# Two-layer hybrid backbone: output products in two 64-row halves, modulation columns one round later, half of two rounds' readout weights on VectorE

## The reference

```python
sh1, sc1, g1, sh2, sc2, g2 = split(silu(c) @ w_mod[layer] + b_mod[layer], 6)   # and for c_ctx
# state-space layer, per group and direction: state 64 complex, 16 channels
states = scan(lam_bar, B_bar @ u)                   # forward in time, and backward
y = real(C_fwd @ states_fwd) + real(C_bwd @ states_bwd) + d_skip * u
q, k = rope(rmsnorm(q)), rope(rmsnorm(k))           # per head, on latent tokens
```

## Time and profile before

| | |
|---|---|
| median of 3 runs | 1943.32 us (1941.05 to 1944.64) |
| profiled execution, its own time | 1942.77 us |
| span of that execution, first to last instruction | 1941.1 us |
| mean granted clock of TensorE (1 is 2.4 GHz) | 0.952 |
| busy: TensorE, weight loads, VectorE, ScalarE, GpSimd | 91%, 55%, 34%, 21%, 17% of the span |
| readout loop from z(1) to the first scores, first and second layer | 133.6 us, 115.3 us |
| chain that ended last, by engine | TensorE 61%, DMA 11%, VectorE 10%, SyncE's queue 6%, GpSimd 5% |

### The profile page before, as it was taken

One profiled execution on the slowest core, in us unless ns is written; L12 is line 12 of the kernel. 1 busy time (PEld: TensorE's weight loads), 2 busy tenths in 40 slices (PEclk: granted clock), 3 DMA queues, 4 the chain that ended last, 5 costly groups with the idle time before them and its releaser, 6 DMA issues.

```text
span 1941.1 us, 25808 instructions
## 1 busy us (share of the span) xinstructions
PE 1762.7 (91%) x9800; PEld 1064.2 (55%) x9800; DVE 656.6 (34%) x1410; ACT 411.4 (21%) x846; POOL 337.1 (17%) x314
## 2 busy tenths in 40 slices
PE   5999998889999999999979798999789999997796
PEld 2567555554444444555546446766458886554463
DVE  4669442660110113211101367775281113110012
ACT  3111111552000003222212231111152002221122
POOL 0004352870000001100000110425291000000000
PEclk9999897999999999999999898999699999999898
DMA  9313258309221243699999421144543367999992
GB/s 387 109 44 114 76 189 296 85 23 349 106 108 65 94 188 130 250 389 345 387 395 388 140 86 66 44 168 139 196 63 126 135 250 280 346 383 394 386 380 89
DMA packets 113523, 397.32 MB, mean 205 GB/s; under 512 B 42992, under 2 KB 62448, under 8 KB 74256
## 3 DMA queue, kind: packets, MB, share of 16 engines
q1 hardware_dynamic: 55920, 327.04, 43.8%
q10 hardware_dynamic: 50720, 29.54, 6.2%
q0 software_dynamic: 6784, 39.33, 6.0%
HBM read 369.65 MB, written 38.80 MB: 210 GB/s over the span
## 4 chain that ended last, share of the span: by engine, by line
PE 61%; DMA 11%; DVE 10%; SPq 6%; POOL 5%; issue 4%; ACT 2%; ACTq 1%; POOLq 0%; DVEq 0%
PE tile_ps L547 54%; SPq L492 6%; DMA arena<-sorted_in 4%; PE turn_ps L547 4%; DMA ring<-in_wpack 3%; POOL arena L1724 2%; DMA vn<-in_wpack 2%; PE out_ps L547 1%; ACTq L1086 1%; DMA arena<-arena 1%; PE turn_ps L772 1%; DVE arena L1592 1%; DVE x L1659 1%; DMA x<-in_xT 1%; DVE rstd L1365 1%
## 5 line engine op out<-in xcount | busy, mean ns | idle before, releaser
L547 PE MATMUL tile_ps<-h,ring 128*128 128x512 f32 (+1 forms) x1312 | 471.9, 514 | 3.9 <-ACT h L965 1.9
L547 PEld LDWEIGHTS tile_ps<-h,ring 128*128 128x128 f32 x1312 | 249.1, 192 | 214.1 <-issue 198.8
L547 PE MATMUL tile_ps<-arena 64*16 64x128 f32 (+4 forms) x1984 | 257.4, 376 | 31.2 <-ACT arena L1180 11.4
L547 PE MATMUL tile_ps<-arena,ring 128*128 128x512 f32 (+1 forms) x704 | 235.4, 486 | 2.7 <-issue 2.7
L547 PEld LDWEIGHTS tile_ps<-arena 128*64 128x64 f32 (+3 forms) x1984 | 165.1, 162 | 95.1 <-issue 64.9
L547 PEld LDWEIGHTS tile_ps<-arena,ring 128*128 128x128 f32 x704 | 133.9, 190 | 96.3 <-issue 87.4
L1724 POOL TENSOR_SCALAR arena<-arena,smx 128x512 f32<-128x512 f32 (+1 forms) x96 | 129.0, 1360 | 81.4 <-DVE smx L1578 81.1
L547 PE MATMUL tile_ps<-ring,arena 128*64 128x256 f32 (+1 forms) x624 | 97.4, 454 | 11.3 <-ACT arena L1180 7.1
L1156 ACT ACTIVATE arena<-tile_ps 128x512 f32<-128x512 f32 (+1 forms) x56 | 27.4, 490 | 347.4 <-PE tile_ps L547 347.4
L1650 DVE TENSOR_TENSOR arena<-tile_ps,arena 64x256 f32<-64x256 f32 x40 | 16.6, 416 | 225.0 <-ACT arena L1177 225.0
L1613 DVE TENSOR_TENSOR arena<-tile_ps,arena 128x512 f32<-128x512 f32 (+1 forms) x32 | 17.9, 558 | 212.1 <-PE tile_ps L547 212.1
(11 more groups left out here) (272 smaller groups left out, 2259.1 us busy)
## 6 DMA issues: line engine op xcount, KB each, us to landing
ring<-in_wpack SPq DMA_DIRECT2D x176, 1024.0 KB, 8.5
arena<-in_wpack SPq DMA_DIRECT2D x64, 1024.0 KB, 17.4
h<-in_wpack SPq DMA_DIRECT2D x15, 1024.0 KB, 26.0
qa<-in_wpack SPq DMA_DIRECT2D x12, 1024.0 KB, 14.7
qn<-in_wpack SPq DMA_DIRECT2D x12, 1024.0 KB, 17.1
kn<-in_wpack SPq DMA_DIRECT2D x12, 1024.0 KB, 20.0
vn<-in_wpack SPq DMA_DIRECT2D x12, 1024.0 KB, 22.1
sorted_out<-arena ACTq DMA_DIRECT2D x80, 128.0 KB, 7.5
```

Of the source, the lines that this page charges most:

```text
L547: return nc.tensor.matmul(out, lhsT, rhs, start=start, stop=stop)
```

## The change

Three things are changed.

1. The Toeplitz product of y is cut into its two halves of 64 rows: `lower` into bank `y`, `upper` into bank `yb`. Each group now has six products of 64 rows in place of one of 128 and four of 64, and the first into `yb` is no longer that with `cp`.
2. `mc` of a round's block moves to the round behind it, right after y there (in round 8, ahead of y), and `mr` moves behind the projection. The blocks of the second layer that rounds 5 to 7 make have `mr` behind the moved `mc` and their own `mc` behind that, ahead of the round's own `mr`; the one that stood in the attention moves to round 8. VectorE's and ScalarE's parts move along, and so do the banks and the order of the ring's slots.
3. For rounds 6 and 7 (`SHARED`) GpSimd makes the real part of `cp` with three products, and VectorE the imaginary part with three more of 128 x 640 (`readout_part`). z(6) and z(7) wait for both.

```diff
-IN_ROUND = {5: 0, 6: 1, 7: 2}
-IN_STEP = {1: 3}
+IN_ROUND = {5: 0, 6: 1, 7: 2, 8: 3}
+def next_mod(l, q):
+    return [IN_ROUND[q]] if l + 1 < LAYERS and q in IN_ROUND else []
+SHARED = (6, 7)
...
     # tile_jobs, the loop of rounds
             names += [(l, "z", q, 0), (l, "z", q, 1)] if q < NQ else []
-            names += [(l, "y", q - 1), (l, "yb", q - 1)] if q else []
+            late = [(l, "mc", MOD1 + q - 1)] if q else []
+            late += [(l + 1, "mr", n) for n in next_mod(l, q)]
+            out = [(l, "y", q - 1), (l, "yb", q - 1)] if q else []
+            names += out + late if q < NQ else late + out
             names += [(l, "qk_ms", q)] if q <= KW else []
+            names += [(l + 1, "mc", n) for n in next_mod(l, q)]
+            names += in_loop(fill, q)
             names += [(l, "mr", MOD1 + q)] if q < NQ else []
-            names += in_loop(fill, q)
-            names += [(l, "mc", MOD1 + q)] if q < NQ else []
             names += [(l, "rope", q)] if q <= KW else []
...
     # TensorE
+                def late_modulation(q):
+                    modulation_columns(l, MOD1 + q - 1)
+                    for n in next_mod(l, q):
+                        modulation(l + 1, n, l)
...
                         pe.wait_ge(cp_done, l * NQ + q + 1)
+                        if q in SHARED:
+                            pe.wait_ge(cp_other, l * len(SHARED) + SHARED.index(q) + 1)
...
-                            mm(bank(fwd)[:, cols], tm[:, o % 2, g, :], ug[:, G, :], True, False)
+                            for d, to in ((lower, fwd), (upper, bwd)):
+                                mm(bank(to)[:, cols], tm[d, o % 2, g, :], ug[d, G, :], True, False)
...
-                                b = mm(bank(bwd)[:, cols], co[upper], s, r == 0, r == 1)
+                                b = mm(bank(bwd)[:, cols], co[upper], s, False, r == 1)
...
     # VectorE
+            def readout_part(q):
...
+                TT(out, pv[1], cv[0], ALU.mult)
+                link(TT(tmp, pv[0], cv[1], ALU.mult))
+                TT(out, out, tmp, ALU.subtract).then_inc(cp_other, 1)
...
+                    if q + 1 in SHARED:
+                        wait_full(dve, (l, "y", q - 1))
+                        readout_part(q + 1)
...
     # GpSimd
+                    if q in SHARED:
+                        TT(o0, o0, ctmp, ALU.add).then_inc(cp_done, 1)
+                    else:
```

More of the change, by code:

```diff
@@ L158, in slot_steps @@
         steps += projected(job)
-    for q in range(NQ):
-        steps += mod(l, MOD1 + q)
+    for q in range(NQ + 1):
+        for n in next_mod(l, q):
+            steps += mod(l + 1, n)
         for job in in_loop(fill, q):
             steps += projected(job)
-        if l + 1 < LAYERS and q in IN_ROUND:
-            steps += mod(l + 1, IN_ROUND[q])
-    if l + 1 < LAYERS:
-        for n in sorted(IN_STEP):
-            steps += mod(l + 1, IN_STEP[n])
+        if q < NQ:
+            steps += mod(l, MOD1 + q)
     for kind, *at in mix_order():
@@ L732, in _ @@
                         product((l, "qk_ms", q), [(c("head_mean"), qsq[:, t:])], bank((l, "qk_ms", q))[:, t:])
-                    if q < NQ:
-                        modulation(l, MOD1 + q, l)
+                    for n in next_mod(l, q):
+                        modulation_columns(l + 1, n)
                     for job in in_loop(fill, q):
@@ L737, in _ @@
                     if q < NQ:
-                        modulation_columns(l, MOD1 + q)
+                        modulation(l, MOD1 + q, l)
                     if q <= KW:
@@ L742, in _ @@
                         product((l, "rope", q), [(c("rot"), v)], bank((l, "rope", q))[:, 0:LAT])
-                    if l + 1 < LAYERS and q in IN_ROUND:
-                        modulation(l + 1, IN_ROUND[q], l)
-                        modulation_columns(l + 1, IN_ROUND[q])
                 us = pairs[l]
@@ L761, in _ @@
                                                         qq[a:a + HD, q0:q0 + P], kk[a:a + HD, 0:nk]))
-                    early = l + 1 < LAYERS and n in IN_STEP
-                    if early:
-                        modulation(l + 1, IN_STEP[n], l)
                     if LAG <= n < len(us) + LAG:
@@ L1086, in _ @@
                             act.dma_start(tm[j * GRP:(j + 1) * GRP, q % 2], zs[:, :, a:a + P]).then_inc(tm_in, 16)
+                    if q == NQ:
+                        for n in next_mod(l, q):
+                            copy_rows(l + 1, n)
                     if q:
@@ L1093, in _ @@
                             head_squares(l, q + 1, c0)
+                    for job in in_loop(fill, q):
+                        copy_projection(job, c0)
                     if q < NQ:
                         copy_rows(l, MOD1 + q)
[L1096 to L1099 removed]
                 for q in range(NQ):
```

42 lines of the change are left out of this document (22 added, 20 removed).

## The result

The changed kernel takes 1960.13 us (median of 4 runs, 1957.76 to 1964.19) against 1943.16 us (4 runs) before: a ratio of 1.009, 95% interval 1.0071 to 1.011. It is slower by 17 us where 12 us less were forecast. Its profiled execution has a span of 1958.6 us and a mean granted clock of 0.945 (0.952 before).

A forecast was written before the change was run, and what follows sets the result against it. TensorE, busy for 91% of the span, was taken to bound the kernel. Gains of 7.5 and 8.3 us less losses of 2.4 and 1.1 gave 12.3 us less, 1931.0 us on the median; likeliest case 1924 to 1936, wider range 1918 to 1942.

The forecast's parts named there:

- The term for low clock in rounds 1 to 4: Rounds 1 to 4: 8.5 us for low clock, 6.1 in the first layer and 2.4 in the second.
- The term for the loads in the first layer's rounds 5 to 8: Two ring slots asked for earlier there: priced at nothing, and at up to 5.5 us if that fails.
- the path from z(6) to z(7) in the second layer: z(7) would come 13.5 us after z(6) in place of 16.9: 3.4 us less.
- signs named for "right": y(4) 2.7 us; projection waits over 2; first-layer rounds at least 18.6; second-layer z(6) 12 behind z(5); first transpose 8 behind scores.
- Output products: y in each round: six pairs per group take 2.7 us, 1.3 less; at low clock 5.1 in place of 6.5.
- The fourth rival: y's 64-row halves don't run side by side, so y gains 0.4 us per round: 1934 us, chance 0.04.
- The floor: Rounds 1 to 4: a round can't be shorter than 18.6 us in the first layer, 15.2 in the second.
- the second rival: Waits of 2.7 us for ScalarE's copy keep TensorE at 1.2 GHz through projection and `mr`: 1948 us, chance 0.09.
- the first rival: The clock stays up with the shorter y; rounds 1 to 4 take 74.4 and 60.0 us: 1919 us, chance 0.15.
- Rounds 5 to 8, second layer: With VectorE sharing GpSimd's products, z(6), z(7) and y(7) gain 2.9, 3.4 and 1.2 us: 7.5 us in all.
- Rounds 5 to 8, first layer: DMAs land 2.3 us earlier, path to the scores 0.8 less, block gone from attention 5.2: 8.3 us in all.
- The third rival: z(6), z(7) come early, but y's DMAs land as before and VectorE's products run beside GpSimd's: 1940 us, chance 0.14.

The follow-up runs named there:

- e1: The kernel before with only y's output product cut into two 64-row halves: 1933.33 us, against 1943 for the kernel before.
- e5: The kernel before with y in halves in both layers and VectorE's three readout products in the second layer alone: 1929.92 us.
- e6: The changed kernel without VectorE's products (`SHARED = ()`), keeping halves and late modulation: 1968.2 us, ratio 1.0105 to the kernel before.
- e7: The changed kernel with second-layer modulation blocks in rounds 5 to 8 using weights already in the ring, 8 loads of 1 MB fewer: 1946.2 us.
- e3: The changed kernel with y's 128-row product and without VectorE's products, so only the moved modulation stays: 1955.29 us.
- e2: The kernel before with only half of the readout weights of rounds 6 and 7 made on VectorE: 1940.3 us.

## Why the prediction was wrong

Three terms of the sum failed. The term for low clock in rounds 1 to 4 was 8.5 us in the two layers and measured 17.9. The term for the loads in the first layer's rounds 5 to 8, put at nothing, hid the largest miss: that stretch took 12.0 us more than forecast. And the path from z(6) to z(7) in the second layer, 13.5 us in the sum, took 19.5, since it left out a wait for the DMAs into `tm`. Most of the signs named for "right" were there even so (y, the waits for the copy, rounds of over 18.6 us, z(6) 12 us behind z(5)), and the clock of rounds 1 to 4 was 0.87 and 0.85, not 0.75 or less: the signs tested the parts that were priced, not those that were left out.

**Output products: right.** From z to `mc` or `qk_ms` are 4.7 us, not 5.8: y gives 1.1 us a round where 1.3 were forecast (2.86 for 2.7 us). At low clock y takes 5.3 us (5.1 forecast, 6.5 before). The fourth rival is out: the 48 loads of a y take less than the 40 before. Weight loads of TensorE in round 3 of the first layer:

```profile
242.15 2.76 PEld L552 LDWEIGHTS tile_ps<-arena 64*128 64x128 f32 x48 [0.21 <-issue]
```

The Trainium skill, TensorE: Matmul & The Clock Gate, section LDWEIGHTS, says that a load costs by its columns and not by its rows. For single loads the trace of the kernel before agrees: two of 64 rows, one in each half and side by side, take 0.19 us, and so does one of 128. What is out is the sum by that rule, in which each of the 48 would have its place behind the last:

```profile
276.70 0.19 PEld L547 LDWEIGHTS tile_ps<-arena 64*128 64x128 f32 x2
...
277.33 0.19 PEld L547 LDWEIGHTS tile_ps<-arena 128*128 128x128 f32 x1
```

**Rounds 1 to 4: the mechanism right, the term for low clock wrong.** The floor held: the waits for the copy are 10.3 us in four rounds (4 x 2.7 = 10.8 forecast). Above the floor of 4 x 18.6 = 74.4 us I put 6.1 for low clock, "since low clock now falls in part on idle time". Measured are 10.7. Of the 22.8 us at 1.2 GHz only 3.0 fell on idle time; the other 19.8, half of them lost, are 9.9 of the 10.7. In rounds 2 and 3 the clock fell at about the end of the wait (in round 3 from 249.9 to 253.3, and the projection begins at 250.03), in round 1 in its middle, in round 4 ahead of it, from 267.0 on, during `qk_ms`; each time the low stretch reached into the projection, the longest work of the round. In the second layer the same term was 2.4 and is 7.2 us, though some 5.4 of 20.5 fell on idle time. The four projections there take 5.38 to 5.68 us, not 3.5 to 3.7. It was the second rival's mechanism in part: the low clock took only part of each projection, and `mr` ran at full clock (1.92 us). Its price of 25.6 us is measured as 17.9, and its total of 1948 us was passed because rounds 5 to 8 lost as well.

**The step that was not taken.** The prediction found the wait and priced it, but treated the round as given. In the order of before the shorter y keeps the clock at 2.4 GHz (e1 and e5, the first rival's mechanism, worth 7.8 and 3.4 us in the profiled executions), with waits of 1.4 to 1.8 us. The late order makes them up to 3.2 us, as `mc` with 0.9 us stands where `mr` with 1.9 stood, and takes the clock away again (e6, the same halves in the late order: 19.8 and 27.3 us at 1.2 GHz). That turned the sign in rounds 1 to 4.

**Rounds 5 to 8, second layer: half right.** z(6) starts 12.1 us after z(5) (12.0 forecast), and VectorE's products for it take 0.82 us each (0.86 forecast), in the timeline of VectorE:

```profile
1372.38 0.81 DVE L1361 TENSOR_TENSOR arena<-arena 128x640 f32<-128x640 f32 x1
1373.11 0.82 DVE L1362 TENSOR_TENSOR arena<-arena 128x640 f32<-128x640 f32 x1
1373.96 0.82 DVE L1363 TENSOR_TENSOR arena<-arena 128x640 f32<-128x640 f32 x1
```

But z(6) to z(7) takes 19.5 us, not 13.5, and y(5) waits 3.95 of them for `tm`'s DMAs. I never asked what stood behind the wait on GpSimd, and what the new times of the slots do to it. Before, SyncE asked for its four loads when `tm`'s issues of round 5 had all begun; now it asks ahead of them. Timelines of ScalarE and SyncE in the second layer, with the line of the DMA view that ends in the median us from issue to landing of these eight, before:

```profile
1350.49 5.12 ACTq L1086 DMA_DIRECT2D arena<-arena  x8
1355.38 2.26 SPq L492 DMA_DIRECT2D ring<-in_wpack  x4
arena<-arena ACTq DMA_DIRECT2D x8, 32.0 KB, 2.0
```

and after:

```profile
1361.54 2.41 SPq L497 DMA_DIRECT2D ring<-in_wpack  x4
1365.90 5.54 ACTq L1095 DMA_DIRECT2D arena<-arena  x8
arena<-arena ACTq DMA_DIRECT2D x8, 32.0 KB, 9.5
```

A median of 2.0 us from issue to landing became 9.5. And two of VectorE's products for z(7) ran beside GpSimd's and took 1.37 and 2.16 us (the sign of "over 1.5 us", seen once); z(7) at 1394.43 starts 0.1 us behind the last of the three:

```profile
1390.02 1.37 DVE L1361 TENSOR_TENSOR arena<-arena 128x640 f32<-128x640 f32 x1
1391.31 2.16 DVE L1362 TENSOR_TENSOR arena<-arena 128x640 f32<-128x640 f32 x1
1393.50 0.82 DVE L1363 TENSOR_TENSOR arena<-arena 128x640 f32<-128x640 f32 x1
```

**Rounds 5 to 8, first layer: wrong.** z(6) came 13.6 us after z(5) (13.5 forecast), and taking the block out of the attention gave 6.5 us (5.2 forecast). The sentence that failed is "I price this at nothing, and at up to 5.5 us": the slots' new times bring some 11 us of DMA into the stage, twice the bound, and nine kernels with them took 57.2 to 67.3 us from z(5) to the first scores, where 52.3 were forecast. I had counted block 3's loads and not those that round 4 no longer makes, and looked for DMAs that land earlier (2.3 us) in a stage that the loads fill. That the loads are what fills it is shown by e7 (51.1 us without eight of them); how many of the 12.0 us each part of it took is not. The third rival had y wait for DMAs, at 1940 us, but let them land when they did; they landed later.

## What to carry to other kernels

When a stage gets shorter, price the wait that takes its place twice: its length, and TensorE's work behind it at the lower clock, unless a row shows that work at full clock behind such a wait. A copy that empties a bank doesn't belong behind a row of DMA issues in the same queue: with the late order moving it was worth 26 us, more than any of the three edits. But it then waits for y, and holds the issues: in the order of before the move gained nothing in the whole, so it has to be tried where the issues have time to spare. And where a step moves, follow what it gives back, in bytes per stretch: ring slots returned later moved 2 MB out of a stretch with a DMA share of 0.36 (0.11 without them) into one with 0.77 (0.81 with them and block 3).

## What the hardware showed

- More weight loads can take less time: 48 of 64 rows, by turns in the lower and the upper half, take 2.76 us, 0.058 each, where 40 in mixed shapes took 3.86; a single one takes 0.19 in either shape.
- The clock can fall without idle time (e3, `mc` at 1.87 us behind 6 us of z and y of small shapes) and doesn't have to with it (e1 and e5, waits of 1.4 to 1.8 us a round, 0 us at 1.2 GHz; in the changed kernel waits of 1.4 to 3.2 us, with 22.8 and 20.5 us at 1.2 GHz).
- `tm`'s eight small DMAs land 13.2 us behind the start of their last issue with four 1 MB loads asked for ahead of them and more among them, 8.8 with eight of the stage's other fourteen loads gone; with the loads held back behind them, TensorE waits 5.2 us for the loads.
- VectorE's 128 x 640 product takes 0.82 us alone; in e2, beside GpSimd's in the first layer, three took 1.35, 1.95 and 2.04, and in the changed kernel two took 1.37 and 2.16.
